# A two-layer hybrid decoder trunk on one core: other start addresses for the stationary tiles in SBUF

## The chip, the cores and the metric

The kernel is written in Bass for Trainium2 and runs on one core. TensorE (PE) multiplies, VectorE (DVE) and ScalarE (ACT) do the element work, SyncE (SP) issues nearly all DMAs, and GpSimd (POOL) clears one buffer. The metric is the device time of one launch in microseconds; lower is better.

## The reference, cut to what matters

All inputs, weights and outputs are float32. With x of 256 tokens by 1024 channels:

```python
for l in range(2):
    mod = silu(c) @ ada_w[l] + ada_b[l]            # nine rows of 1024: shift, scale, gate of three blocks
    h = modulate(x, 0); x = x + 0.5 * gate(0) * swiglu(h, ffn_wg[l, 0], ffn_wu[l, 0], ffn_wd[l, 0])
    z = modulate(x, 1) @ w_in[l]                   # q, k, v | conv input u | two branch gates
    # 12 heads of 64 in 3 groups (window, dilation) = (128, 1), (512, 4), (2048, 16), rotary, merged by lse
    y_attn = merged_attention(q, k, v) @ attn_wo[l]
    y_conv = silu(layer_norm(depthwise_conv31(glu(u)))) @ conv_wo[l]
    y = sigmoid(g_attn) * y_attn + sigmoid(g_conv) * y_conv
    x = x + gate(1) * (y @ w_out[l])
    h = modulate(x, 2); x = x + 0.5 * gate(2) * swiglu(h, ffn_wg[l, 1], ffn_wu[l, 1], ffn_wd[l, 1])
return rms_norm(x, final_g)                        # modulate: rms_norm * (1 + scale) + shift; d_ff = 2816
```

## The kernel before

All matrices are cut on the host into 200 panels of 128 x 2048 float32 (1 MB). SP streams them, one DMA a panel, into a ring of six buffers, `raw`. Most panels are split into two parts of type fp32r: ScalarE casts `raw` to `w_hi` (a ring of five, L708), and VectorE writes the rest, `raw - w_hi`, over the raw panel as `w_lo` (helper `minus`, L997). The activations are split in the same way into `hA_hi` and `hA_lo` (normalised input), `hB_hi` and `hB_lo` (the merged branches), `mid_hi` and `mid_lo` (hidden part of an FFN), `end_hi` and `end_lo` (the last such part of an FFN), `o_hi` and `o_lo` (attention output). A product is then three fp32r matmuls, hi x hi, hi x lo, lo x hi (helper `three`, L329 to L331). In each, a 128 x 128 piece of an activation tile is the stationary operand, loaded by a LDWEIGHTS of its own, and 512 columns of a panel are the moving operand. 24 panels aren't split: they are multiplied in plain float32 with `hF` as the stationary operand (L348).

The order of the instructions on each engine is written out by hand, and semaphores join the engines. Between the matmuls stand PE transposes: L396 (`mid`), L380 (`xn_h`, `xn_q`), L476 (`glu`), L485 (`roped`), L526 (`probs`), L558 (`work`), L636 (`ln_xn`), L663 (`y`). The data to be turned is their stationary operand. The convolution is 480 VectorE operations (L1186), which read `conv_in` at a moving offset and add onto `work`.

The change is in how SBUF is laid out. `room(nbytes, phase)` hands out bytes one after the other; with a phase it first moves on until the address, counted from the first byte of the whole area, is `phase` modulo 512. `raw`, `w_hi`, `x` and `hF` come first and have sizes that are multiples of 512, so they all begin at phase 0. Every piece of a stationary tile is 512 bytes long in a partition and begins a multiple of 512 from its tile's start, and every moving piece of a panel begins a multiple of 1024 from the panel's start: so a tile's phase is that of all its pieces.

Of the kernel before, what the change touches and what calls it, by code (L numbers as in the profile page):

```python
# [10 lines left out]
F32R = mybir.dt.float32r  # L11
BF16 = mybir.dt.bfloat16

P = 128
D = 1024
T = 256
DEPTH = 2
KC = D // P
# [93 lines left out]
def decoder_program(nc, x_in, c_row, g_row, params, rope, ident, mask, ada_w, weights, out):  # L112
    with ExitStack() as ctx:
# [3 lines left out]
        def at(offset, name, shape, dt=F32):  # L117
            return nc.alloc_sbuf_tensor_at(name, shape, dt, offset=offset)

        def room(nbytes, phase=None):  # L120

            o = top[0]
            if phase is not None:
                o += (base + phase - o) % 512
            top[0] = o + (nbytes + 31) // 32 * 32
            return o

        def sb(name, shape, dt=F32):
            n = 2 if dt == BF16 else 4
            for s in shape[1:]:  # L130
                n *= s
            return at(room(n), name, shape, dt)
# [8 lines left out]
        w_hi = sb("w_hi", [P, HI, PW], F32R)  # L141
        x = sb("x", [P, TT, D])
        hF = sb("hF", [P, KC, T])
        hA_at = room(2 * KC * T * 4, 0)
        hA_hi = at(hA_at, "hA_hi", [P, KC, T], F32R)
        hA_lo = at(hA_at + KC * T * 4, "hA_lo", [P, KC, T], F32R)
        c_bc = sb("c_bc", [P, D])
# [29 lines left out]
        y = at(qk_at, "y", [P, TT, D])  # L177
        xn_q = at(qk_at, "xn_q", [P, TT, D])
        ada_raw = at(work_at, "ada_raw", [P, ADA_RING, D])
        att_at = room(16896, 0)  # L180
        v_sb = at(att_at, "v_sb", [P, TT, NG * 256])
        probs = [at(att_at + 6144, "probs0", [P, NG, P]), at(att_at + 7680, "probs1", [P, NG, T])]
        o_sb = at(att_at + 7680, "o_sb", [P, TT, 256])
# [2 lines left out]
        hB_lo = at(att_at + 8192, "hB_lo", [P, KC, T], F32R)  # L186
        xn_h = at(att_at + 8192, "xn_h", [P, TT, D])
        ln_xn = at(att_at, "ln_xn", [P, TT, D])
        gates_at = room(16384, 0)
        gates = at(gates_at, "gates", [P, TT, 2 * D])  # L190
        rope_a = at(gates_at, "rope_a", [P, TT, 512])
        rope_b = at(gates_at + 4096, "rope_b", [P, TT, 512])
# [3 lines left out]
        mid_hi = at(gates_at + 4096, "mid_hi", [P, 2, T], F32R)  # L196
        mid_lo = at(gates_at + 6144, "mid_lo", [P, 2, T], F32R)

        end_hi = at(gates_at + 8192, "end_hi", [P, 2, P], F32R)
        end_lo = at(gates_at + 9216, "end_lo", [P, 2, P], F32R)  # L200
        product = at(gates_at + 8192, "product", [P, 2, D])
        glu_at = room(4096)
        sg = at(glu_at, "sg", [P, TT, 256])
        glu = at(glu_at + 2048, "glu", [P, TT, 256])
        o_hi = at(att_at, "o_hi", [P, 2, T], F32R)
        o_lo = at(att_at + 2048, "o_lo", [P, 2, T], F32R)
        ctx.enter_context(nc.sbuf_tensor("slab", [P, top[0] - base], mybir.dt.uint8, align_bytes=32))

        ps = ctx.enter_context(nc.psum_tensor("ps", [P, 8, 512], F32))
# [1254 lines left out]
```

## Time and profile before

| | us |
|---|---|
| median of 3 runs | 1296.38 |
| lowest and highest run | 1295.26 and 1297.17 |
| the profiled execution | 1295.26 |
| its span, first to last instruction | 1293.5 |

| engine | busy us | share of the span |
|---|---|---|
| PE, matmul | 1238.3 | 96% |
| PE, weight load (beside the matmuls) | 957.3 | 74% |
| VectorE | 965.1 | 75% |
| ScalarE | 547.3 | 42% |

The span leaves out about 1.8 us around the instructions. Matmuls are pipelined, so the duration of one (0.39 us) is longer than the distance from its start to the next one's; where the text speaks of a gap it is this distance, from start to start. The mean granted clock of TensorE is 0.994 of full speed.

### The profile page before, as it was taken

To read this page: it belongs to the slowest core of one execution; us is meant where nothing else is said; L and a number is where in the kernel's file an instruction comes from. 1 tells how busy PE (TensorE), PEld (TensorE's weight loads), DVE (VectorE), ACT (ScalarE), POOL (GpSimd) and SP (SyncE) were. 2 spreads that over 40 slices of the span, in tenths; PEclk is the share of its full clock that TensorE was granted. 3 is DMA by queue.
4 is the path that set the end of the run, shared out by engine and by line. 5 is a ranking of instruction groups with operands and counts; after the bars stand their busy time and mean duration, and the time that the engine had idled before them with its cause. 6 is when DMAs were issued, how large, how long until landed. Compare 5 with 4: busy or idle time off the path is not lost.

```text
span 1293.5 us, 13852 instructions
## 1 busy us (share of the span) xinstructions
PE 1238.3 (96%) x5448; PEld 957.3 (74%) x5448; DVE 965.1 (75%) x1341; ACT 547.3 (42%) x576; POOL 2.2 (0%) x5
## 2 busy tenths in 40 slices
PE   3999999999998999999999999999999899999997
PEld 2588887765765787888878888876676677888885
DVE  5698886699996576988668888669999856744443
ACT  3353344532345365344354443354233454644331
POOL 0000000000000000000000000000000000000000
PEclk9999999999999999999999999999999899999999
DMA  9989994454323339889747899454432334555540
GB/s 374 417 316 378 372 377 169 163 183 159 130 98 130 137 124 376 340 340 358 294 180 280 340 343 357 174 188 174 175 130 98 130 130 169 190 190 178 204 177 33
DMA packets 52913, 293.44 MB, mean 227 GB/s; under 512 B 6640, under 2 KB 6896, under 8 KB 27120
## 3 DMA queue, kind: packets, MB, share of 16 engines
q1 hardware_dynamic: 51120, 289.38, 60.0%
q10 hardware_dynamic: 1728, 3.17, 0.7%
q8 instruction: 43, 0.70, 0.2%
q14 instruction: 22, 0.18, 0.0%
HBM read 291.45 MB, written 1.07 MB: 226 GB/s over the span
## 4 chain that ended last, share of the span: by engine, by line
PE 89%; DVE 4%; DMA 3%; ACT 2%; issue 1%; SPq 0%; DVEq 0%
PE ps L329 23%; PE ps L331 23%; PE ps L330 23%; PE ps L348 13%; DMA raw<-in_weights 2%; PE ps L537 1%; PE ps L515 1%; PE ps L396 1%; DMA ada_raw<-in_ada_w 1%; DVE w_lo L997 1%; DVE hF L1084 1%; PE ps L526 0%; PE ps L485 0%; ACT L714 0%; DVE hA_lo L997 0%
## 5 line engine op out<-in xcount | busy, mean ns | idle before, releaser
L997 DVE TENSOR_TENSOR w_lo<-raw,w_hi 128x2048 fp32r<-128x2048 f32 x176 | 401.1, 2287 | 37.6 <-ACT w_hi L708 37.3
L708 ACT CAST w_hi<-raw 128x2048 fp32r<-128x2048 f32 x176 | 334.5, 1910 | 176.8 <-DMA raw<-in_weights 113.7
L329 PE MATMUL ps<-w_hi,hA_hi 128*128 128x512 f32 (+1 forms) x992 | 395.9, 399 | 5.8 <-DVE hA_lo L997 5.8
L331 PE MATMUL ps<-w_hi,hA_lo 128*128 128x512 f32 (+1 forms) x992 | 384.3, 387 | 0.0
L330 PE MATMUL ps<-w_lo,hA_hi 128*128 128x512 f32 (+1 forms) x992 | 383.6, 387 | 0.0
L329 PEld LDWEIGHTS ps<-w_hi,hA_hi 128*128 128x128 f32 x992 | 186.9, 188 | 49.8 <-issue 15.1
L331 PEld LDWEIGHTS ps<-w_hi,hA_lo 128*128 128x128 f32 x992 | 186.7, 188 | 39.0
L330 PEld LDWEIGHTS ps<-w_lo,hA_hi 128*128 128x128 f32 x992 | 187.0, 189 | 37.9 <-issue 2.9
L1186 DVE SCALAR_TENSOR_TENSOR work<-conv_in,par,work 128x256 f32<-128x256 f32 x480 | 193.9, 483 | 0.0
L1012 DVE SCALAR_TENSOR_TENSOR product<-ada_raw,c_bc 128x1024 f32<-128x1024 f32 x144 | 171.7, 1220 | 16.0 <-DMA ada_raw<-in_ada_w 15.6
L348 PE MATMUL ps<-raw,hF 128*128 128x512 f32 x384 | 172.0, 600 | 5.5 <-ACT hF L733 5.5
L348 PEld LDWEIGHTS ps<-raw,hF 128*128 128x128 f32 x384 | 72.1, 193 | 87.0 <-issue 86.8
L329 PE MATMUL ps<-w_hi,mid_hi 128*128 128x512 f32 x336 | 131.3, 391 | 2.3 <-DVE mid_lo L997 2.3
L330 PE MATMUL ps<-w_lo,mid_hi 128*128 128x512 f32 x336 | 130.8, 389 | 0.0
L331 PE MATMUL ps<-w_hi,mid_lo 128*128 128x512 f32 x336 | 130.8, 389 | 0.0
L997 DVE TENSOR_TENSOR mid_lo<-ps,mid_hi 128x512 fp32r<-128x512 f32 (+1 forms) x44 | 29.3, 667 | 106.7 <-ACT mid_hi L770 103.3
L763 ACT ACTIVATE act<-ps 128x512 f32<-128x512 f32 (+1 forms) x48 | 27.0, 563 | 136.6 <-PE ps L331 131.7
L329 PEld LDWEIGHTS ps<-w_hi,mid_hi 128*128 128x128 f32 x336 | 63.1, 188 | 15.9 <-DVE mid_lo L997 3.0
L770 ACT CAST mid_hi<-ps 128x512 fp32r<-128x512 f32 x40 | 23.4, 586 | 120.5 <-PE ps L396 120.5
L331 PEld LDWEIGHTS ps<-w_hi,mid_lo 128*128 128x128 f32 x336 | 63.1, 188 | 13.2
L330 PEld LDWEIGHTS ps<-w_lo,mid_hi 128*128 128x128 f32 x336 | 63.1, 188 | 12.9
L1100 DVE TENSOR_TENSOR mid<-act,ps 128x512 f32<-128x512 f32 (+1 forms) x48 | 30.9, 643 | 45.1 <-ACT act L763 45.1
(121 smaller groups left out, 749.7 us busy)
## 6 DMA issues: line engine op xcount, KB each, us to landing
raw<-in_weights SPq DMA_DIRECT2D x200, 1024.0 KB, 4.9
ada_raw<-in_ada_w SPq DMA_DIRECT2D x144, 512.0 KB, 7.5
gate_bc<-gate_scratch ACTq DMA_DIRECT2D x6, 512.0 KB, 6.4
x<-in_x_tok SPq DMA_DIRECT2D x1, 1024.0 KB, 7.6
out_tok<-xn_h SPq DMA_DIRECT2D x4, 256.0 KB, 2.2
c_bc<-in_c_row SPq DMA_DIRECT2D x1, 512.0 KB, 4.6
c_bc<-in_g_row SPq DMA_DIRECT2D x1, 512.0 KB, 5.6
mask_all<-in_mask SPq DMA_DIRECT2D x1, 416.0 KB, 16.6
```

Source lines behind the costliest of these rows:

```text
L329: nc.tensor.matmul(out_ap, stat[0], mov[0], start=start, stop=False)
L330: nc.tensor.matmul(out_ap, stat[0], mov[1], start=False, stop=False)
L331: return nc.tensor.matmul(out_ap, stat[1], mov[0], start=False, stop=stop)
L348: mm = nc.tensor.matmul(out_ap, hF[:, k, t], raw[:, p % RAW, c], start=(k == 0), stop=(k == KC - 1))
L396: mm = nc.tensor.transpose(ps[:, bank, c:c + P], mid[:, tt, kk * P:(kk + 1) * P], ident_sb[:])
L708: nc.scalar.copy(w_hi[:, s % HI, :], raw[:, p % RAW, :]).then_inc(hi_done, 1)
L763: nc.scalar.activation(act[:, tts[0]:tts[-1] + 1, :], ps[:, bank + tts[0]:bank + tts[-1] + 1, 0:256], ACT.Silu).then_inc(silu_done, 1)
L770: nc.scalar.copy(mid_hi[:], cols(bank)).then_inc(mid_hi_done, 1)
L997: return nc.vector.tensor_tensor(dst, whole, hi_part.bitcast(F32), ALU.subtract)
L1012: nc.vector.scalar_tensor_tensor(out=product[:, q % 2, :], in0=ada_raw[:, q % ADA_RING, :], scalar=1.0, in1=c_bc[:], op0=ALU.mult, op1=ALU ...
L1100: nc.vector.tensor_tensor(mid[:, c, :], act[:, c, :], ps[:, bank + tts[0]:bank + tts[-1] + 1, 256:512], ALU.mult).then_inc(mid_done, 1)
L1186: nc.vector.scalar_tensor_tensor(out=work[:, c, :], in0=conv_in[:, c, t:t + T], scalar=par[:, o:o + 1], in1=work[:, c, :], op0=ALU.mult, o ...
```

## The change

It gives phases to the rooms that hold the stationary tiles, which had phase 0, and moves two pairs of tiles inside their rooms. All rooms behind them move on too. No instruction is added, removed, or put in another place: what each engine runs, in which order and with which waits, is word for word the same.

```diff
-        hA_at = room(2 * KC * T * 4, 0)
+        hA_at = room(2 * KC * T * 4, 384)
...
-        att_at = room(16896, 0)
+        att_at = room(16896, 448)
...
-        gates_at = room(16384, 0)
+        gates_at = room(16384, 320)
...
-        end_hi = at(gates_at + 8192, "end_hi", [P, 2, P], F32R)
-        end_lo = at(gates_at + 9216, "end_lo", [P, 2, P], F32R)
+        end_hi = at(gates_at + 8192 + 160, "end_hi", [P, 2, P], F32R)
+        end_lo = at(gates_at + 9216 + 160, "end_lo", [P, 2, P], F32R)
...
-        o_hi = at(att_at, "o_hi", [P, 2, T], F32R)
-        o_lo = at(att_at + 2048, "o_lo", [P, 2, T], F32R)
+        o_hi = at(att_at + 480, "o_hi", [P, 2, T], F32R)
+        o_lo = at(att_at + 480 + 2048, "o_lo", [P, 2, T], F32R)
```

What this makes of the phases (bytes modulo 512 from the start of the area, worked out from the sizes in the code):

| tiles | role | before | after |
|---|---|---|---|
| `raw`, `w_lo`, `w_hi` | moving operand of L329 to L331 and L348 | 0 | 0 |
| `hF`, `x` | stationary operand of L348; residual | 0 | 0 |
| `hA_hi`, `hA_lo` | stationary, fp32r | 0 | 384 |
| `hB_hi`, `hB_lo` (also `xn_h`, `ln_xn`) | stationary, fp32r (the latter: of transposes) | 0 | 448 |
| `mid_hi`, `mid_lo` (also `mid`, `roped`, `glu`) | stationary, fp32r (the latter: of transposes) | 0 | 320 |
| `end_hi`, `end_lo` | stationary, fp32r | 0 | 480 |
| `o_hi`, `o_lo` | stationary, fp32r | 0 | 416 |
| `work`, `y`, `xn_q`, `qkT`, `ada_raw` | element work, transposes, DMA | 352 | 224 |
| `conv_in` | element work | 416 | 288 |
| `ident_sb` | moving operand of the transposes | 448 | 320 |

The area grows by 832 bytes a partition.

## Rows read from the trace of the kernel before

**Rows 1.** The page, sections 1 and 4: engines, chain that ended last.

```profile
PE 1238.3 (96%) x5448; PEld 957.3 (74%) x5448; DVE 965.1 (75%) x1341; ACT 547.3 (42%) x576; POOL 2.2 (0%) x5
...
PE 89%; DVE 4%; DMA 3%; ACT 2%; issue 1%; SPq 0%; DVEq 0%
```

**Rows 2.** Groups by form: line, op, out<-in, shapes xcount | busy us, mean ns | idle before.

```profile
L329 PE MATMUL ps<-w_hi,hA_hi 128*128 128x512 f32 x960 | 386.7, 403 | 5.8 <-DVE hA_lo L997 5.8
...
L329 PE MATMUL ps<-w_hi,mid_hi 128*128 128x512 f32 x336 | 131.3, 391 | 2.3 <-DVE mid_lo L997 2.3
...
L329 PE MATMUL ps<-w_hi,hB_hi 128*128 128x512 f32 x64 | 26.0, 407 | 5.4 <-DVE hB_lo L997 5.4
...
L329 PE MATMUL ps<-w_hi,o_hi 128*128 128x512 f32 x16 | 7.1, 441 | 0.0
L329 PE MATMUL ps<-w_hi,end_hi 128*128 128x512 f32 x16 | 6.6, 414 | 0.8 <-DVE end_lo L997 0.8
```

**Rows 3.** Timeline of PE, undisturbed fp32r stream: start us, duration us, instruction.

```profile
800.67 0.39 PE L329 MATMUL ps<-w_hi,mid_hi 128*128 128x512 f32 x1
...
805.88 0.39 PE L331 MATMUL ps<-w_hi,mid_lo 128*128 128x512 f32 x1
```

**Rows 4.** Timeline of PE around a turn of `mid` at 605 us.

```profile
605.30 0.60 PE L396 MATMUL ps<-ident_sb,mid 128*128 128x128 f32 x4
605.65 0.48 PE L329 MATMUL ps<-w_hi,hA_hi 128*128 128x512 f32 x1
605.97 0.40 PE L330 MATMUL ps<-w_lo,hA_hi 128*128 128x512 f32 x1
...
608.51 0.39 PE L329 MATMUL ps<-w_hi,hA_hi 128*128 128x512 f32 x1
```

**Rows 5.** Timeline of PE, 256-column fp32r stream.

```profile
326.23 0.28 PE L331 MATMUL ps<-w_hi,hA_lo 128*128 128x256 f32 x1
...
328.87 0.28 PE L329 MATMUL ps<-w_hi,hA_hi 128*128 128x256 f32 x1
```

**Rows 6.** Timeline of PE, bf16 matmuls of 512 and 256 columns.

```profile
323.31 0.38 PE L507 MATMUL ps<-mask_all 128*128 128x512 bf16 x1
323.53 0.27 PE L509 MATMUL ps<-mask_all 128*128 128x256 bf16 x1
```

**Rows 7.** Chain in order of time: start us, us, what.

```profile
251.26 6.87 PE ps L348 x16
...
434.18 0.87 PE ps L663 x8
...
1037.83 0.87 PE ps L636 x8
```

**Rows 8.** Weight loads of transposes by line: duration ns min/median/max.

```profile
L380 PEld LDWEIGHTS ps<-ident_sb,xn_q x32: 139/141/142, 464.7 to 1106.8; 128*128 128x128 f32 x32
...
L663 PEld LDWEIGHTS ps<-ident_sb,y x32: 139/141/142, 433.8 to 1079.8; 128*128 128x128 f32 x32
...
L396 PEld LDWEIGHTS ps<-ident_sb,mid x176: 138/139/143, 53.0 to 1279.6; 128*128 128x128 f32 x176
```

**Rows 9.** The convolution's operations; then groups by form, ScalarE and VectorE.

```profile
L1186 DVE SCALAR_TENSOR_TENSOR work<-conv_in,par,work x480: 472/481/504, 250.0 to 1029.5; 128x256 f32<-128x256 f32 x160
...
L721 ACT ACTIVATE xn_h<-x 128x1024 f32<-128x1024 f32 x10 | 10.5, 1055 | 11.4 <-DVE x L1065 9.9 <-DMA x<-in_x_tok 1.4
...
L721 ACT ACTIVATE xn_q<-x 128x1024 f32<-128x1024 f32 x4 | 4.2, 1061 | 12.2 <-DVE x L1065 12.2
```

**Rows 10.** Two stretches of the convolution in the timeline of VectorE.

```profile
257.00 4.44 DVE L1186 SCALAR_TENSOR_TENSOR work<-conv_in,par,work 128x256 f32<-128x256 f32 x11
...
389.99 4.04 DVE L1186 SCALAR_TENSOR_TENSOR work<-conv_in,par,work 128x256 f32<-128x256 f32 x10
```

**Rows 11.** Issues of DMA: KB each, median us from issue to landing.

```profile
ada_raw<-in_ada_w SPq DMA_DIRECT2D x144, 512.0 KB, 7.5
...
c_bc<-in_c_row SPq DMA_DIRECT2D x1, 512.0 KB, 4.6
c_bc<-in_g_row SPq DMA_DIRECT2D x1, 512.0 KB, 5.6
```

**Rows 12.** Timeline of all engines: a matmul and the weight load beside it.

```profile
249.98 0.39 PE L329 MATMUL ps<-w_hi,hA_hi 128*128 128x512 f32 x1
249.98 0.19 PEld L330 LDWEIGHTS ps<-w_lo,hA_hi 128*128 128x128 f32 x1
```

## The prediction, made before the changed kernel ran

> **What bounds the kernel now.** I read the page's engine line and chain first. PE is busy 1238.3 us of a span of 1293.5 us, and the chain that ended last is PE to 89%, with VectorE at 4%, DMA at 3% and ScalarE at 2% [rows 1]. So the time is nearly the number of matmuls times the gap between them. Nothing else comes close.
>
> Next the groups by form, to see which matmuls these are. 128 x 512 fp32r matmuls come in threes, so each row for L329 stands for three groups: 3 x (960 + 336 + 64 + 16 + 16) = 4176 [rows 2]. Every one of them has its stationary operand in a tile whose phase changes. The other large group, plain float32 against `hF` (L348), has both operands where they were.
>
> Then the timeline, for the gap. In an undisturbed stretch the reader is to see 24 starts from 800.67 to 805.88 us, so 23 gaps in 5.21 us, 226.5 ns each [rows 3]. 4176 of these are 946 us, 73% of the span. That product is the lever of the change: 1 ns on the gap is 4.2 us.
>
> **The change, part by part.** Instructions, waits and DMAs are the same, in the same order. So the sum has only terms in which an instruction or a transfer takes another time because its tile lies elsewhere. The trace of before has no fp32r weight load at another phase than 0, so no row prices the main term; it has to be bounded.
>
> *The fp32r gap.* What could an address do to it? While 512 columns of the panel stream, the next 512-byte piece of the activations is loaded. Both reads come from SBUF, and before, both begin at phase 0. Three readings bear on it.
>
> First, the size of what is there to win or lose. 512 columns at 2.4 GHz (the granted clock is full in this stretch) are 213.3 ns; the gap is 226.5, so 13.2 ns a matmul are not columns. A bf16 matmul of 512 columns is followed by the next start after 0.22 us (323.31 to 323.53) [rows 6]. In plain float32, 16 records take 6.87 us, 429.4 ns each against 426.7 ns for their columns at that clock, only 2.7 ns over [rows 7]. So the 13 ns belong to fp32r alone.
>
> Second, whether they look like two reads in each other's way. With 256 columns the gap is 22 gaps in 2.64 us (326.23 to 328.87), 120.0 ns against 106.7 ns of columns: again 13.3 ns over [rows 5]. It is a fixed price of an instruction, the same when the next weight load overlaps half as many columns. That speaks for a start-up of the instruction rather than for reads that collide along the stream, but it doesn't prove it: the weight load is equally long in both cases.
>
> Third, whether phase matters to weight loads elsewhere. Transposes do have stationary operands at two phases. `mid` lies at 0, and `y` and `xn_q` at 352: weight loads 139 ns in the median for the one, 141 for the others [rows 8]. Eight turns of `ln_xn` (phase 0) and eight of `y` (phase 352) both take 0.87 us [rows 7]. So 352 bytes do nothing to a transpose. [...]
>
> One row does show that the fp32r gap isn't always the same at equal addresses. After a turn of `mid`, 11 gaps from 605.97 to 608.51 us take 2.54 us, 230.9 ns each, and only then do they settle at 226.5 [rows 4]. So relative timing inside PE costs up to 4.4 ns a gap, and the settled stream is free of it. Where timing matters, an address may.
>
> Bounds for this term: down, the columns and the 2.7 ns of float32, 216.0 ns, which fits the bf16 gap of 0.22 us: 10.5 ns x 4176 = -44 us. Up, the unsettled gap for good: 4.4 ns x 4176 = +18 us. The nearest rows are the transposes, which show nothing at all, so I take 0.
>
> [...]
>
> *The price of breaks.* The unsettled stretch of [rows 4] costs 11 x 4.4 = 48 ns. The `mid` turns alone are 176 / 4 = 44 [rows 8], and with other transposes and the float32 panels there are roughly 100 breaks in the stream. If half are of this kind, that is 2.4 us in all, at most 4.8. New phases could remove or double it: -3 to +3 us. I take 0, as I have no reason for a sign.
>
> *Transposes.* Their stationary tiles go from 0 to 320 or 448, or from 352 to 224, and `ident_sb` from 448 to 320. By rows 8 and the two of rows 7 the cost is 0.
>
> *VectorE and ScalarE.* `w_lo` and `w_hi` casts, the largest groups of both engines, don't move. Of the others, a squaring into `xn_h` (phase 0) takes 1055 ns and one into `xn_q` (352) 1061 [rows 9]: 0.6%. The convolution's 480 operations read `conv_in` at a shift of four bytes a tap, and chunk to chunk at 1144 bytes, so they scan the phases by themselves: 472, 481 and 504 ns at the minimum, median and maximum [rows 9]. Early in a layer 11 of them take 4.44 us, and late, in other channels, 10 take 4.04 us: 404 ns both, as successive ones overlap [rows 10]. If all the spread were of addresses, the 6% of the chain on these engines (78 us) would change by -2% to +5%, -1.5 to +3.9 us. I take 0. What is off the chain hides behind PE; only VectorE's chain around the convolution is tight enough to matter, and its cover is bounded by these same 3.9 us.
>
> *DMA.* `ada_raw`, `c_bc` and the parameters land elsewhere; the 200 panels do not. All moves are multiples of 32 bytes and every row written stays in one piece. Two loads of `c_bc` of the same size took 4.6 and 5.6 us [rows 11]; one such load on the start-up path would be -1 to +1 us. I take 0.
>
> Sum: 0 us against the profiled execution, 1295.26 us (span 1293.5 and 1.8 around it). That run was the lowest of three and lies 1.1 us under their median, so I forecast the median, 1296.4 us.
>
> **The rivals.**
>
> *The settled stream is lost (slower).* Place: the weight load beside each fp32r matmul of L329 to L331. Before, both reads run with equal phase; if it is the equal phase that lets the stream settle, then with 384, 448 and 320 against 0 it stays at the unsettled gap. For it: the gap after breaks, at which the same instructions take 4.4 ns more, and that the settled gap is the lower one. Against: the transposes, and that all pieces return to the same gap although they lie many multiples of 512 apart. Price: up to +18 us, 1314 us; it decides the sign from 0.6 ns a gap on (2.6 us). Since `hA` carries 2880 of the 4176, a loss there alone would be 13 us.
>
> *The fixed 13 ns are the two reads that begin together at the same phase (much faster).* The weight load for the next matmul starts with the matmul beside it, both at 249.98 us [rows 12]. If they meet in the same place of SBUF and one waits, another phase frees both: 1296.4 - 44 = 1252 us. For it: only fp32r pays, and it reads the most bytes a cycle. Against: the sum is fixed to 0.1 ns over 256 and 512 columns, which a start-up explains as well.
>
> *A part of it goes (faster).* The breaks settle at once (-3 us), or up to 2 ns leave the gap: -3 to -11 us, 1285 to 1293 us, with 1290 in the middle. Same evidence as before, at a size which no row excludes.
>
> *The change does nothing at all* is not a rival here but the forecast: the addresses do change, and the rows give no engine that notices.
>
> **How the numbers follow.** A measurement of this kernel tells from no change what is beyond 0.2%, 2.6 us. Forecast, no visible effect: 0.48, with its own range of 1293.5 to 1299.5 (the terms of VectorE, DMA and breaks don't add up in one direction). Settled stream lost in whole or part: 0.21. A part gained: 0.24. The full 44 us: 0.07. From these, faster is 0.24 + 0.07 = 0.31, same is 0.48, slower is 0.21. The range of 8 in 10 takes all of the forecast, nearly all of the small gain and half of the loss: 1284 to 1308 us. It leaves out the full gain and the upper half of the loss.
>
> **What would show it.** If right, the stretch that starts near 800 us again has gaps of 226.5 ns, the 256-column stream 120.0, the transposes 0.87 us for eight, and PE's busy time is within 3 us of 1238.3. The slower rival would show as L330 and L331 gaps of 228 to 231 ns in stretches without breaks, with VectorE and ScalarE durations the same; the faster ones as gaps nearer 216 ns. If the gaps hold and the time still moves, my term for VectorE and ScalarE was wrong, and the convolution's median (481 ns) and PE's waits for VectorE would have moved. A gap that differs between `hA` (384) and `mid` (320) would show a true dependence on phase.

## The result, and the profile after

| | before | after |
|---|---|---|
| median, us (4 runs each) | 1296.04 | 1316.15 |
| profiled execution, us | 1295.26 | 1315.99 |
| its span, us | 1293.5 | 1314.2 |
| PE busy, us | 1238.3 | 1260.4 |

The change makes the kernel slower: the ratio is 1.0153, 95% interval 1.0136 to 1.0171, or 20.1 us. I had forecast no change, 1296.4 us, and the time lies outside my range of 1284 to 1308. It is 2.2 us above the first rival's price, 1314 us.

The page of the changed kernel, sections 1 and 4, answers to [rows 1]:

```profile
PE 1260.4 (96%) x5448; PEld 959.5 (73%) x5448; DVE 965.6 (73%) x1341; ACT 546.3 (42%) x576; POOL 2.2 (0%) x5
...
PE 89%; DVE 4%; DMA 3%; ACT 2%; issue 2%; SPq 0%; DVEq 0%
```

PE is busy 22.1 us longer at the same number of instructions. VectorE (+0.5 us) and ScalarE (-1.0 us) aren't. The groups by form answer to [rows 2] (count, busy us, mean ns, idle before):

```profile
L329 PE MATMUL ps<-w_hi,hA_hi 128*128 128x512 f32 x960 | 391.1, 407 | 5.5 <-DVE hA_lo L997 5.5
...
L329 PE MATMUL ps<-w_hi,mid_hi 128*128 128x512 f32 x336 | 133.6, 398 | 1.9 <-DVE mid_lo L997 1.9
```

The duration of one has grown by 4 and 7 ns, and PE waits no longer for VectorE than before (5.5 against 5.8, 1.9 against 2.3). So it isn't a new wait. The timeline of PE around the same place in the program shows what it is; answer to [rows 3]:

```profile
811.82 0.40 PE L329 MATMUL ps<-w_hi,hA_hi 128*128 128x512 f32 x1
...
814.62 0.40 PE L329 MATMUL ps<-w_hi,mid_hi 128*128 128x512 f32 x1
...
819.99 0.39 PE L331 MATMUL ps<-w_hi,mid_lo 128*128 128x512 f32 x1
```

From 811.82 to 814.62 are 12 gaps with `hA`, 233.3 ns each; from 814.62 to 819.99 are 23 with `mid`, 233.5 ns each. Before, the same place had 226.5. What is left to compare is the 256-column stream, the convolution and the squarings, answers to [rows 5] and [rows 9]:

```profile
331.14 0.28 PE L330 MATMUL ps<-w_lo,hA_hi 128*128 128x256 f32 x1
...
333.99 0.28 PE L330 MATMUL ps<-w_lo,hA_hi 128*128 128x256 f32 x1
```

```profile
L1186 DVE SCALAR_TENSOR_TENSOR work<-conv_in,par,work x480: 475/481/498, 254.3 to 1043.9; 128x256 f32<-128x256 f32 x160
```

```profile
L721 ACT ACTIVATE xn_h<-x 128x1024 f32<-128x1024 f32 x10 | 10.5, 1054 | 11.2 <-DVE x L1065 10.0 <-DMA x<-in_x_tok 1.2
...
L721 ACT ACTIVATE xn_q<-x 128x1024 f32<-128x1024 f32 x4 | 4.3, 1064 | 12.3 <-DVE x L1065 12.3
```

The stream of 256 columns has 24 gaps in 2.85 us, 118.8 ns, where it had 120.0: it lost nothing, and even gained a little. The convolution's median is still 481 ns. Only the 512-column fp32r gap has moved.

Does that account for the time? I took all gaps between 220 and 245 ns that begin with a 512-column fp32r matmul, some 4000 in either trace, and summed what they are over 226.67 ns: 3.5 us before, 24.3 us after. The difference, 20.8 us, is the size of the loss in the profiled span (1314.2 - 1293.5 = 20.7 us). That the two agree to 0.1 us is in part luck. All start-to-start distances behind the 4176 matmuls, the long ones at breaks and at half clock included, add up to 990.2 us before and 1012.4 after, 22.2 us more. Between 400 and 1100 us the granted clock falls to 0.50 four times in the trace after and three times before, for 3.4 us each time; fp32r matmuls of 512 columns then start 427 ns apart. And the distances behind L348, L537 and L558 are 1.5 us shorter after.

### The profile page after: what moved, and what is told of

It reads as the page before. It is cut to its first block, busy times and chain, and to the rows that moved or that the text cites. A ratio compares the mean times of both kernels' runs of the same rounds, so it can differ in the third digit from the quotient of the medians.

```text
span 1314.2 us, 13852 instructions
## 1 busy us (share of the span) xinstructions
PE 1260.4 (96%) x5448; PEld 959.5 (73%) x5448; DVE 965.6 (73%) x1341; ACT 546.3 (42%) x576; POOL 2.2 (0%) x5
## 4 chain that ended last, share of the span: by engine, by line
PE 89%; DVE 4%; DMA 3%; ACT 2%; issue 2%; SPq 0%; DVEq 0%
PE ps L329 24%; PE ps L330 23%; PE ps L331 23%; PE ps L348 12%; DMA raw<-in_weights 2%; PE ps L515 1%; PE ps L396 1%; PE ps L537 1%; DMA ada_raw<-in_ada_w 1%; DVE hF L1084 1%; PE ps L485 0%; ACT L714 0%; PE ps L526 0%; DVE w_lo L997 0%; DVE hA_lo L997 0%
## 5 line engine op out<-in xcount | busy, mean ns | idle before, releaser
L329 PE MATMUL ps<-w_hi,hA_hi 128*128 128x512 f32 (+1 forms) x992 | 400.3, 404 | 5.5 <-DVE hA_lo L997 5.5
L331 PE MATMUL ps<-w_hi,hA_lo 128*128 128x512 f32 (+1 forms) x992 | 389.3, 392 | 0.0
L330 PE MATMUL ps<-w_lo,hA_hi 128*128 128x512 f32 (+1 forms) x992 | 389.2, 392 | 0.0
L329 PEld LDWEIGHTS ps<-w_hi,hA_hi 128*128 128x128 f32 x992 | 187.5, 189 | 53.7 <-issue 14.7
L331 PEld LDWEIGHTS ps<-w_hi,hA_lo 128*128 128x128 f32 x992 | 187.4, 189 | 42.9
L348 PE MATMUL ps<-raw,hF 128*128 128x512 f32 x384 | 171.4, 598 | 5.5 <-ACT hF L733 5.5
L329 PE MATMUL ps<-w_hi,mid_hi 128*128 128x512 f32 x336 | 133.6, 398 | 1.9 <-DVE mid_lo L997 1.9
L348 PEld LDWEIGHTS ps<-raw,hF 128*128 128x128 f32 x384 | 71.7, 192 | 86.7 <-issue 86.5
L331 PE MATMUL ps<-w_hi,mid_lo 128*128 128x512 f32 x336 | 132.7, 395 | 0.0
L329 PEld LDWEIGHTS ps<-w_hi,mid_hi 128*128 128x128 f32 x336 | 63.2, 188 | 17.8 <-DVE mid_lo L997 2.6
L331 PEld LDWEIGHTS ps<-w_hi,mid_lo 128*128 128x128 f32 x336 | 63.2, 188 | 15.4
```

The lines of the kernel that those rows point to most:

```text
L329: nc.tensor.matmul(out_ap, stat[0], mov[0], start=start, stop=False)
L330: nc.tensor.matmul(out_ap, stat[0], mov[1], start=False, stop=False)
L331: return nc.tensor.matmul(out_ap, stat[1], mov[0], start=False, stop=stop)
L348: mm = nc.tensor.matmul(out_ap, hF[:, k, t], raw[:, p % RAW, c], start=(k == 0), stop=(k == KC - 1))
```

## The experiments

The question was what about the addresses does this: their difference to the panels, their absolute place, or the traffic of other engines, whose tiles moved as well. Then, whether another layout would be better than the one before.

### The stream alone, at many phases

A kernel in which PE runs only the threes of the fp32r stream, with one stationary and one moving buffer, read at chosen offsets. VectorE and ScalarE have finished filling them at 18.5 us, when PE starts.

```diff
+            for o, st, mv, a, z in seq(0, 0): nc.tensor.matmul(o, st, mv, start=a, stop=z)
+            for o, st, mv, a, z in seq(0, 0): nc.tensor.matmul(o, st, mv, start=a, stop=z)
+            for o, st, mv, a, z in seq(0, 32): nc.tensor.matmul(o, st, mv, start=a, stop=z)
...
```

> A stream of fp32r matmuls alone, in the threes of the kernel (hi hi, hi lo, lo hi; 128 x 128 stationary, 512 columns moving), nothing else of the kernel and no other engine at work: it computes nothing of the reference. Each pair of code lines is one setting, 48 matmuls: moving phase 0, 384 or 128 bytes, stationary phase 0 to 480 in steps of 32; then 16, 48, 80, 400; then 256 columns at 0, 128, 256, 384. Theory 1 (the two reads of PE meet, by the difference of their phases): gap 226.7 ns where the phases are equal, at each of the three moving phases, and 230 to 236 at differences of 320, 384, 448. Theory 2 (the absolute phase of the stationary tile decides): the same curve over the stationary phase at all three moving phases. Theory 3 (traffic of ScalarE, VectorE and DMA at other phases disturbs PE): 226.7 ns at every setting here.

Timeline of PE, one row for each code line of 24 matmuls, so a gap is the distance between the starts of two rows over 24. L70 to L72 pass from 0, 256 to 0, 288; L78 is 0, 384; L87 is 384, 0; L110 is 384, 384:

```profile
109.91 5.60 PE L70 MATMUL ps<-moving,still 128*128 128x512 f32 x24
115.35 5.61 PE L71 MATMUL ps<-moving,still 128*128 128x512 f32 x24
120.80 5.76 PE L72 MATMUL ps<-moving,still 128*128 128x512 f32 x24
126.39 5.76 PE L73 MATMUL ps<-moving,still 128*128 128x512 f32 x24
...
154.43 5.75 PE L78 MATMUL ps<-moving,still 128*128 128x512 f32 x24
160.01 5.74 PE L79 MATMUL ps<-moving,still 128*128 128x512 f32 x24
165.59 5.76 PE L80 MATMUL ps<-moving,still 128*128 128x512 f32 x24
...
204.57 5.76 PE L87 MATMUL ps<-moving,still 128*128 128x512 f32 x24
210.17 5.76 PE L88 MATMUL ps<-moving,still 128*128 128x512 f32 x24
...
332.64 5.60 PE L110 MATMUL ps<-moving,still 128*128 128x512 f32 x24
338.08 5.61 PE L111 MATMUL ps<-moving,still 128*128 128x512 f32 x24
343.52 5.76 PE L112 MATMUL ps<-moving,still 128*128 128x512 f32 x24
```

(338.08 - 332.64) / 24 = 226.7 ns at 384 with 384, and (160.01 - 154.43) / 24 = 232.5 ns at 0 with 384. The mean of the 23 gaps within the second row of each setting, in ns, by the difference of the two phases (the same to 0.2 ns at moving phases 0, 128 and 384, and with 256 added, but for the one setting named below):

| stationary minus moving, modulo 256 | 0 | 32 | 64 | 96 | 128 | 160 | 192 | 224 |
|---|---|---|---|---|---|---|---|---|
| gap, ns | 226.7 | 233.4 | 233.5 | 234.6 | 232.3 | 233.4 | 228.8 | 233.3 |

The exception is moving 384 with stationary 0, a difference of 128: (210.17 - 204.57) / 24 = 233.3 ns, where five other settings of the same difference had 232.3. Another is a stationary phase of 400, which is a difference of 144: it had 233.1 ns here, and 144 will have 226.7 below. So the difference doesn't fix the gap alone; I come back to that.

It settles the question all the same. Theory 1 holds, the difference counts, with a period of 256 bytes that I had not foreseen. Theory 2 falls, since the stationary tile at 384 is fast with a panel at 384 or 128. Theory 3 falls: no other engine is at work here, and the loss is there in full. With 256 columns no such loss appears (119.8, 119.9, 120.0 and 118.6 ns at 0, 128, 256, 384).

### One part of the change at a time

```diff
-        hA_at = room(2 * KC * T * 4, 0)
+        hA_at = room(2 * KC * T * 4, 384)
```

> Only hA has phase 384; all else has the phases of before. Theories 1 and 2: the gap of the matmuls with hA (2880 of them) is 232 ns as in the changed kernel, that of mid stays 226.7: 2880 x 5 ns = 14 us, 1310 to 1312 us. Rival (the lengthening is of mid and its neighbours, or of the break after each turn): under 1300 us.

The other way round, the changed kernel with that one line set back:

```diff
-        hA_at = room(2 * KC * T * 4, 384)
+        hA_at = room(2 * KC * T * 4, 0)
```

> The changed kernel with hA back at phase 0. Theories 1 and 2: the gap of hA is 226.7 again, that of mid stays at 233: 1296 + 1008 x 6.5 ns = 1302 to 1304 us. If the terms do not add up, hA's stream is disturbed by its neighbours and it stays above 1308.

| kernel | median, us | ratio to before (95%) | mean gap, `hA` and `mid`, ns |
|---|---|---|---|
| only `hA` moved | 1309.35 | 1.0106 (1.0081 to 1.0131) | 232.6 and 228.5 |
| all but `hA` | 1302.51 | 1.0054 (1.0034 to 1.0073) | 227.9 and 233.3 |
| before, in those runs | 1296.21 | | 227.7 and 226.9 |

(The mean gaps are of all gaps from 220 to 245 ns, in the profiled execution.) The losses are 13.1 and 6.3 us, and their sum of 19.4 is the 20.1 of the whole change within the uncertainty. The moved tile has the long gap, the other hardly. `mid` at 228.5 ns beside a moved `hA` pays a little: in a run of 24 `mid` matmuls behind `hA` the first gaps are 236, 224, 231, 236, 228, 232, 231 ns, and only then 227. So two parts counted alone pay more than both together. Summed over the gaps of the traces, only `hA` costs 15.2 us and all but `hA` 7.4, together 22.7 against 20.8 for the whole change. In both profiled executions the granted clock fell to half only twice between 400 and 1100 us, and three times in the one before, so their spans hide a part of this. My 1310 to 1312 was 1 us high for the first, and 1302 to 1304 right for the second.

The changed kernel itself holds three points of the curve: its mean gap is 232.7 ns with `hA` (difference 128 modulo 256), 233.3 with `mid` (64) and 229.3 with `hB` (192), and the stream alone had 232.3 or 233.3, 233.5 and 228.8.

### Equal phases again, elsewhere

```diff
-        top = [base]
+        top = [base + 384]
-        hA_at = room(2 * KC * T * 4, 0)
+        hA_at = room(2 * KC * T * 4, 384)
-        att_at = room(16896, 0)
+        att_at = room(16896, 384)
-        gates_at = room(16384, 0)
+        gates_at = room(16384, 384)
```

> Everything, the panels included, stands 384 bytes further on: stationary and moving tiles have equal phases again, all at 384 of the area. Theory 1: time and gap of before, 1296 us and 226.7 ns. Theory 2: the stationary tiles are where they were slow, so 1314 to 1318 us.

Then two kernels like the one before, in which those three rooms have phase 256 (or, in the second, 192), while the panels stay at 0:

```diff
-        hA_at = room(2 * KC * T * 4, 0)
+        hA_at = room(2 * KC * T * 4, 256)
-        att_at = room(16896, 0)
+        att_at = room(16896, 256)
-        gates_at = room(16384, 0)
+        gates_at = room(16384, 256)
```

> The kernel before with all stationary fp32r tiles at phase 256. If only the difference modulo 256 counts, as the stream alone says: 1296 us, gap 226.7 ns. If the rule needs equal phases modulo 512: as in the changed kernel, 1310 us or more.

> All stationary fp32r tiles at phase 192. The stream alone had 228.8 ns there, against 226.7: 4176 x 2.1 = 8.8 us, so 1305 us. If the kernel's other engines shape the cost, it need not follow the stream alone: 1310 or more, as at the other unequal phases.

| kernel | median, us | before, in those runs | ratio (95%) |
|---|---|---|---|
| all at 384, panels too | 1295.98 | 1296.21 | 1.0004 (0.9992 to 1.0016) |
| stationary at 256 | 1296.36 | 1295.71 | 1.0007 (0.9995 to 1.0019) |
| stationary at 192 | 1302.23 | 1295.71 | 1.0050 (1.0031 to 1.0069) |

In the first, the 23 gaps at the place of [rows 3] take 5.21 us, as before:

```profile
799.69 0.39 PE L331 MATMUL ps<-w_hi,hA_lo 128*128 128x512 f32 x1
...
804.90 0.39 PE L330 MATMUL ps<-w_lo,mid_hi 128*128 128x512 f32 x1
```

So the whole kernel follows the stream alone: no loss at differences of 0 and 256, and a third of the loss at 192. There I expected 8.8 us and measured 6.5. The trace has 10.3 us over 226.67 ns a gap, against 3.5 before, so 6.8 us more. My product set 228.8 ns against a stream that is always settled, which the one before isn't: it pays 3.5 us after its breaks already, and those stretches lose little more.

### The two parts apart, other types, and the turns

The stream alone again, with a phase for each of moving hi and lo, and stationary hi and lo; then plain float32; then four transposes ahead of the aligned stream.

```diff
+            for o, st, mv, a, z in mix(0, 128, 0, 128): nc.tensor.matmul(o, st, mv, start=a, stop=z)
...
+            for o, x, i in turn(0, 448): nc.tensor.transpose(o, x, i)
+            for o, st, mv, a, z in seq(0, 0): nc.tensor.matmul(o, st, mv, start=a, stop=z)
```

> PE alone again, nothing of the reference is computed; each pair of code lines is one setting, 48 matmuls. Here the two parts get phases of their own: moving hi 0, moving lo 128, stationary hi 0, stationary lo 128. Theory A (the load of the next stationary piece meets the running matmul): the pairs that run side by side are then all equal (hi beside hi, lo beside lo), so 226.7 ns. Theory B (the matmul and its own stationary piece matter): two of three pairs differ by 128, so near 231. Moving hi 0, moving lo 128, both stationary at 0: A and B both one pair of three off, 228 to 229. The grid of stationary phases looks for a setting under 226.7; by a model with a floor there is none. Phases 4 to 24: if the rule is by 16 or 32 bytes, 4 and 8 read as 0. Plain float32 at 0, 64, 96, 128: 429 ns a record at all. Turns: four transposes and then the aligned stream, with data at 0 or 352 and the identity at 0, 448, 64, 128, 320: if the unsettled gaps after a turn come from the turn's own phases, they vanish at 0 with 0; if from the interruption, they are the same at all ten.

Timeline of PE: L82 is the aligned stream, L84 has hi with hi and lo with lo equal (0, 128, 0, 128); L164 to L166 are plain float32 at 0 and 64; L172 to L174 are four transposes within the aligned stream:

```profile
25.55 5.60 PE L82 MATMUL ps<-moving,still 128*128 128x512 f32 x24
30.98 5.70 PE L83 MATMUL ps<-moving,still 128*128 128x512 f32 x24
36.52 5.71 PE L84 MATMUL ps<-moving,still 128*128 128x512 f32 x24
42.06 5.76 PE L85 MATMUL ps<-moving,still 128*128 128x512 f32 x24
```

```profile
482.75 7.03 PE L164 MATMUL ps<-plain 128*128 128x512 f32 x16
489.62 7.03 PE L165 MATMUL ps<-plain 128*128 128x512 f32 x16
496.49 7.03 PE L166 MATMUL ps<-plain 128*128 128x512 f32 x16
```

```profile
536.30 5.61 PE L172 MATMUL ps<-moving,still 128*128 128x512 f32 x24
541.75 0.60 PE L173 MATMUL ps<-idt,plain 128*128 128x128 f32 x4
542.11 5.72 PE L174 MATMUL ps<-moving,still 128*128 128x512 f32 x24
```

Neither theory A nor B holds. L84 to L85 is 5.54 us, 230.8 ns, although each matmul runs beside a load of equal phase. Every mixture of multiples of 64 had 228.9 ns or more, and only all parts equal gave 226.7. Nor do single pairs add up: with moving lo alone at 128, for which I expected 228 to 229 ns by either theory, the gap was 233.5. What a row shows instead is a rhythm, a sequence of gaps that repeats, and that is a matter of the three together. Plain float32 is 429.2 ns a record at all four phases, (489.62 - 482.75) / 16.

After a turn the unsettled gaps appear in all ten combinations of phases, for instance 230, 236, 229, 232, 231 and then 227. The same combination, run twice, needed 4 matmuls once and 10 the other time (phases 0 and 448). So they come from the interruption, not from the turn's phases. The same in the kernel, with `ident_sb` and `work_at` put at phase 0:

```diff
-        ident_sb = sb("ident_sb", [P, P])
+        ident_sb = at(room(P * 4, 0), "ident_sb", [P, P])
-        work_at = room(KC * T * 4)
+        work_at = room(KC * T * 4, 0)
```

> The kernel before with the identity, and work, y, xn_q, qkT and ada_raw, at phase 0 as well, so that transposes too have equal phases. If the unsettled gaps after a break (3.6 us in all by the trace) come from the turns' phases: 1293 us. If they come from the interruption itself: no change, within 1 us.

It took 1296.56 us, ratio 1.0005 (0.9995 to 1.0015): no change.

One thing in this scan didn't fit the first: with both stationary parts at 192 the gap was 233.3 ns, not 228.8.

### Shapes, bf16, and the two values at 192

```diff
+            for o, st, mv, a, z in cut(64, 512, 96): nc.tensor.matmul(o, st, mv, start=a, stop=z)
...
+            for o, st, mv, a, z in half(64): nc.tensor.matmul(o, st, mv, start=a, stop=z)
```

> PE alone, nothing of the reference is computed; a pair of code lines is one setting, 48 matmuls, stationary at phase 0, 64 or 128 against moving 0. First stationary pieces of 128, 96, 64 and 32 columns, then moving pieces of 480 to 256 columns, then the threes in bf16, then 192 reached from different settings. If the weight load and the running matmul meet in SBUF, a load of half the columns costs about half (3 ns instead of 6.5 over the aligned gap) and with 32 columns nearly nothing; if instead the start of each matmul is what depends on the phase, the extra is the same at all stationary widths. In both cases bf16, which reads half the bytes, shows 216 ns at every phase. The stream at 192 had 228.8 ns in one scan and 233.3 in another: if it has two steady cycles, both appear here, depending on what ran before.

Timeline of PE; L93 and L94 are 96 stationary columns at phase 128 (L89 and L90: at 0), L139 and L140 the threes in bf16:

```profile
65.17 5.68 PE L89 MATMUL ps<-moving,still 128*96 128x512 f32 x24
70.69 5.68 PE L90 MATMUL ps<-moving,still 128*96 128x512 f32 x24
...
87.18 5.60 PE L93 MATMUL ps<-moving,still 128*96 128x512 f32 x24
92.62 5.60 PE L94 MATMUL ps<-moving,still 128*96 128x512 f32 x24
98.06 5.68 PE L95 MATMUL ps<-moving,still 128*64 128x512 f32 x24
...
298.96 5.34 PE L139 MATMUL ps<-m,s 128*128 128x512 bf16 x24
304.14 5.34 PE L140 MATMUL ps<-m,s 128*128 128x512 bf16 x24
```

Both expectations on the width failed. Narrower loads don't make the gap shorter: 96 columns have 229.9 ns at phase 0 and 226.7 at phase 128, (92.62 - 87.18) / 24; 64 columns have 230.0, 232.9 and 229.3 at 0, 64 and 128; 32 columns 231.6, 231.6 and 230.8. So equal phase is not the rule as such; it is the good setting for loads of 128 columns beside 512 (226.7 ns against 233.4 and 232.3 at 64 and 128). With 256 moving columns the aligned setting is the worst of three (120.0, 117.8, 118.6), with 480 the middle one (216.7, 216.1, 220.0), with 384 the best again (173.3, 176.7, 175.8). Only bf16 came as expected, 215.8 ns at every phase, (304.14 - 298.96) / 24.

The two values at 192 are two steady rhythms of one setting. Reached from phase 0 or 128 it repeats 226, 229, 232; reached from 64 it repeats 234, 233, 233. L154 is 192 after 128, 5.49 us for 24 matmuls, and L158 is 192 after 64, 5.60 us:

```profile
379.59 5.66 PE L154 MATMUL ps<-moving,still 128*128 128x512 f32 x24
385.08 5.76 PE L155 MATMUL ps<-moving,still 128*128 128x512 f32 x24
...
401.88 5.76 PE L158 MATMUL ps<-moving,still 128*128 128x512 f32 x24
407.48 5.62 PE L159 MATMUL ps<-moving,still 128*128 128x512 f32 x24
```

A difference of 128 has two rhythms as well: one with gaps of up to 241 ns, mean 232.3, and one of 229 and 238 in turn, mean 233.3. The changed kernel shows both: of its 92 long stretches with `hA` (18 gaps or more), 49 end in the first and 43 in the second.

### Every four bytes

```diff
+            for o, st, mv, a, z in seq(0, 4): nc.tensor.matmul(o, st, mv, start=a, stop=z)
+            for o, st, mv, a, z in seq(0, 8): nc.tensor.matmul(o, st, mv, start=a, stop=z)
...
```

> PE alone, nothing of the reference is computed: the stream of 512-column threes with the stationary phase from 4 to 252 in steps of 4, then 256 and 0, 48 matmuls each. If equal phases modulo 256 are the only settled point, every value between is over 226.7 ns (by the samples so far, 229 to 235) and there is no layout that beats the one before. If there is a second point, or one under 226.7, it shows here, and a kernel with it would be faster by 4.2 us for each ns.

The last question was whether any layout beats the one before. In the timeline of PE, L161 is 212 bytes, L168 and L169 are 228, L170 and L171 are 232, L178 and L179 are 248, L181 is 252, L182 is 256:

```profile
617.76 5.84 PE L161 MATMUL ps<-moving,still 128*128 128x512 f32 x24
...
656.97 5.60 PE L168 MATMUL ps<-moving,still 128*128 128x512 f32 x24
662.41 5.61 PE L169 MATMUL ps<-moving,still 128*128 128x512 f32 x24
667.86 5.71 PE L170 MATMUL ps<-moving,still 128*128 128x512 f32 x24
673.41 5.71 PE L171 MATMUL ps<-moving,still 128*128 128x512 f32 x24
...
712.23 5.76 PE L178 MATMUL ps<-moving,still 128*128 128x512 f32 x24
717.83 5.76 PE L179 MATMUL ps<-moving,still 128*128 128x512 f32 x24
...
728.86 5.61 PE L181 MATMUL ps<-moving,still 128*128 128x512 f32 x24
734.30 5.62 PE L182 MATMUL ps<-moving,still 128*128 128x512 f32 x24
```

The figures are again means of the 23 gaps within the second row of a setting, here by the stationary phase, against moving 0. Of the 63 phases between 0 and 256 none had a mean under 226.7 ns; 26 had 233.2 to 233.4, and the longest was 236.8, at 212: 5.84 us in the row of L161 less 0.39 for its last matmul, over 23. Six of them had 226.7 here as well: 120, 132, 144, 156, 228 and 252, the last with (734.30 - 728.86) / 24. So my "only settled point" was wrong. But no setting of the 512-column stream, in this scan or the three others, had a mean gap under 226.7, so they showed no better version to build. It changes fast from one phase to the next: 226.7 at 228, (662.41 - 656.97) / 24, and 231.1 at 232, whose first row has (673.41 - 667.86) / 24 = 231.2.

These six are no safe choice. In the scan of pairs, 252 was reached from 244 and ran at 233.3 ns for all its 48 matmuls, and 144 had 233.1 in the first scan. The likely reason is again what ran before; but these scans ran on different chips, so for 144 and 252 this isn't shown, as it is for 128 and 192 within one run. A difference of 0 or 256 came back to 226.7 ns in all four scans, whatever ran before it, after at most eleven matmuls at full clock. A single pass over the phases shows one rhythm for each, and not whether there is a second.

## Why the prediction was wrong

**What bounds the kernel** was right: 20.8 us of longer fp32r gaps are 20.7 us of span. "1 ns on the gap is 4.2 us" held: 4176 x (232.7 - 227.5), the mean gaps after and before, is 21.7 us, against 20.8 summed over the gaps that the traces have.

**The step that failed is the choice in the main term.** I wrote that the nearest rows were the transposes, "which show nothing at all, so I take 0". They were the wrong neighbour. Eight transposes of 128 columns take 0.87 us [rows 7], 0.85 ns a column, where the fp32r stream takes 226.5 ns for 512, 0.44 a column: the moving columns of a transpose pass at half the rate. And the scans show that plain float32 has no dependence on phase at all (429.2 ns at four phases). The nearer row was the one of the same instruction, [rows 4]: equal addresses, equal tiles, and 230.9 ns where the settled stream has 226.5. It said that this stream has a favourable rhythm which can be lost. What the runs showed in place of 0 is +5.2 ns a gap (227.5 to 232.7), 20.8 us. The upper bound I took from that row, 4.4 ns or +18 us, was near the result but too low to be a bound: the last two of its eleven gaps are settled already (227 and 226 ns), and the nine before them have a mean of 231.9, 5.2 over 226.7. I left this rival at a chance of 0.21, and cut half of it out of the range.

**The second argument, a fixed price of 13 ns**, came out for 512 columns, where no setting went under it, but the price isn't fixed. I had set 213.3 ns for 512 columns, 0.4167 ns each, or 2.4 columns a ns. The traces bear this out. The aligned gaps at 512, 384, 320 and 256 columns, 226.7, 173.3, 146.7 and 120.0 ns, lie 0.417 a column apart. And in the trace before, where the granted clock is 0.50, six fp32r gaps take 2.56 us, 426.7 ns each: twice 213.3, with nothing over it:

```profile
1031.99 0.63 PE L331 MATMUL ps<-w_hi,hA_lo 128*128 128x512 f32 x1
...
1034.55 0.50 PE L331 MATMUL ps<-w_hi,hA_lo 128*128 128x512 f32 x1
```

The 426.7 ns for 512 plain float32 columns are 0.833 each, and between its records of 512 and the transposes of 128 columns, 429.4 and 108.8 ns [rows 7], there are 0.835 a column. Over 0.4167 ns a column, at full clock, the aligned stream has 13.3 ns at 512, 384, 320 and 256 columns, 16.7 at 480 and 15.9 at 448, and 256 columns have 11.1 at a difference of 64 bytes (117.8 - 106.7). The two widths that I had rows for, 512 and 256, were of the four that agree. It argued against the fast rival only, whose 44 us no run found. I let it speak for no effect as well, which it can't: that a floor is fixed says nothing on leaving the floor.

**The rival's mechanism** was right in where (L329 to L331), how (no new wait, the gap longer in stretches without breaks) and nearly how much (up to 18 us, and 20.1 measured). It was right in that `hA` carries most of it. That 13.1 us were measured with only `hA` moved, where 13 were forecast, is luck: its gaps grew by 4.9 ns and not 4.4, `mid` beside it by another 1.6, 15.2 us in the trace together, of which the span shows 13.0 with one fall of the clock fewer. The lost stream doesn't stay in the rhythm that follows a break either, as the rival said; each difference has a rhythm or two of its own. Its wording that "it is the equal phase that lets the stream settle" holds for 128-column loads; the shapes and the fine scan show that it isn't a general rule.

**The fast rival** fell: bf16 had its 215.8 ns at each phase here, fp32r with 512 columns never came under 226.7. That fp32r reads the most is so, 2048 bytes a partition in 226.7 ns, against 1024 in 215.8 for bf16 and 2048 in 429.2 for plain float32, but no phase made its gap at 512 columns shorter than the aligned one.

**The terms taken as 0** for transposes, convolution, ScalarE and DMA were right as far as the runs can tell: `work`, `y`, `ident_sb` and `ada_raw` at phase 0 gave 1.0005 (0.9995 to 1.0015), the convolution's median didn't move in the changed kernel, and the distances behind its transposes of `mid`, `roped`, `y` and `xn_h` add up to the same within 0.02 us. No run moved a DMA's tile alone. **The price of breaks** was as estimated, 3.5 us in all against my 2.4, and it doesn't depend on the turns' phases.

**What stays open** is the mechanism inside PE. That it is PE's own is shown (233.4 ns at 32, with no other engine at work), as is the dependence on both reads' phases. Why one rhythm settles and another doesn't is not. Reads that meet in SBUF would fit the period of 256 bytes, but I can't explain by them that narrower loads pay as much (232.9 ns with 64 columns at 64), that pairs of equal phase side by side don't help (230.8 ns), or that one setting has two rhythms (228.8 and 233.3 ns at 192).

## What to carry to other kernels

In a kernel bound by a stream of fp32r matmuls of 512 columns with a fresh load of 128 columns each, keep the stationary pieces and the panels at the same address modulo 256; here it is worth 1.5% and costs 160 bytes of padding (ahead of `att_at`, from phase 352 to 0). The whole kernel was run at differences of 0, 256 and 192, and no run tried the six other phases in it. When a trace shows one instruction at two gaps with nothing to tell them apart, treat that as a sign that the shorter gap can be lost, and price a change of layout by it, not by another kind of instruction that happens to be insensitive. And measure such a stream alone: one run of a small kernel gave the curve that the whole kernel then followed at four differences (0, 64, 128 and 192). Reach each setting from more than one other, since it may have two rhythms.

## What the runs showed of the hardware that I had not expected

- The fp32r gap at 512 columns takes values between 226.7 and 236.8 ns mostly by the difference of the two operands' phases, with a period of 256 bytes, and depends on four bytes more or less (226.7 at 228, 231.1 at 232).
- One setting can have two steady rhythms, by what ran before it: 228.8 and 233.3 ns at a difference of 192, 232.3 and 233.3 at 128. Between scans, 144 had 226.7 and 233.1, and 252 had 226.7 and 233.3.
- After four transposes the aligned stream needed four to eleven matmuls to settle, at all ten combinations of their phases.
- Plain float32 (429.2 ns a record) and bf16 (215.8 ns) showed none of this, at four phases each.
